# A recurrence in six head pairs: T ahead of U in each level, an earlier half split, three k-steps moved into the preparation, other wait counts

## The reference

```python
def step(S, inp):
    r_t, d_t, k_t, v_t, kk_t, b_t = inp
    sa = jnp.einsum('bhij,bhj->bhi', S, -kk_t)
    S = S * d_t[:, :, None, :] + sa[..., None] * b_t[:, :, None, :] + v_t[..., None] * k_t[:, :, None, :]
    return S, jnp.einsum('bhij,bhj->bhi', S, r_t)
...
decay = jnp.exp(-jnp.exp(w))
b = kk * a
...
gates = jax.nn.sigmoid((mg + gate_b).astype(jnp.float32)).reshape(B, S, N_BRANCH, D_MODEL)
```

## Time and profile before

| | us |
|---|---|
| median of 3 runs (range) | 3747.38 (3745.06 to 3751.47) |
| the profiled execution, device time | 3744.87 |
| its span, from the first to the last instruction | 3743.1 |
| PE busy | 3579.6 (96%) |
| DVE, ACT, POOL busy | 2261.2, 1618.1, 434.4 |
| chain that ended last, PE's share | 83% |
| mean granted clock of TensorE | 0.984 |

### The profile page before, as it was taken

One profiled execution on the slowest core, in us unless ns is written; L12 is line 12 of the kernel. 1 busy time (PEld: TensorE's weight loads), 2 busy tenths in 40 slices (PEclk: granted clock), 3 DMA queues, 4 the chain that ended last, 5 costly groups with the idle time before them and its releaser, 6 DMA issues.

```text
span 3743.1 us, 84941 instructions
## 1 busy us (share of the span) xinstructions
PE 3579.6 (96%) x33038; PEld 3520.4 (94%) x33038; DVE 2261.2 (60%) x3089; ACT 1618.1 (43%) x2173; POOL 434.4 (12%) x481
## 2 busy tenths in 40 slices
PE   6999999999999999899999999999999699999996
PEld 6999888889999999889999999999999699999996
DVE  6787666665565477876545454566665554545454
ACT  4456433244444434654434343443444343434343
POOL 5000232300010000312000000020002500000007
PEclk9999999999999999999999999999999899999998
DMA  5544222235655555445555555555455355555553
GB/s 200 164 149 146 92 70 70 77 112 184 200 183 184 186 170 169 147 152 181 182 184 177 190 177 184 178 185 185 158 164 164 111 185 177 189 179 184 177 189 124
DMA packets 165422, 606.24 MB, mean 162 GB/s; under 512 B 18384, under 2 KB 18512, under 8 KB 164992
## 3 DMA queue, kind: packets, MB, share of 16 engines
q1 hardware_dynamic: 163296, 594.62, 49.4%
q10 hardware_dynamic: 1760, 6.80, 0.5%
q0 software_dynamic: 192, 2.23, 0.2%
HBM read 601.47 MB, written 2.10 MB: 161 GB/s over the span
## 4 chain that ended last, share of the span: by engine, by line
PE 83%; DVE 9%; POOL 3%; ACT 2%; issue 2%; ACTq 0%; DVEq 0%; POOLq 0%
PE bank L313 26%; PE bank L314 26%; PE bank L315 25%; PE bank L1187 4%; DVE w_lo L302 2%; POOL ln_acc L2517 1%; POOL ln_acc L2520 1%; POOL ln_d L2515 1%; POOL ln_sq L2518 1%; ACT w_hi L293 0%; ACT X L2557 0%; DVE hx L372 0%; DVE mem_hl L372 0%; DVE xa L1765 0%; PE bank L1393 0%
## 5 line engine op out<-in xcount | busy, mean ns | idle before, releaser
L293 ACT ACTIVATE w_hi<-raw 128x1024 fp32r<-128x1024 f32 x1130 | 1162.1, 1052 | 974.7 <-PE bank L315 957.5
L302 DVE TENSOR_TENSOR w_lo<-raw,w_hi 128x1024 fp32r<-128x1024 f32 x1130 | 1375.0, 1256 | 101.2 <-ACT w_hi L293 101.0
L313 PE MATMUL bank<-u,w_hi 128*128 128x256 f32 (+1 forms) x2304 | 656.9, 285 | 9.6 <-DVE w_lo L302 9.5
L314 PE MATMUL bank<-u,w_hi 128*128 128x256 f32 (+1 forms) x2304 | 658.7, 286 | 0.0
L315 PE MATMUL bank<-u,w_lo 128*128 128x256 f32 (+1 forms) x2304 | 657.5, 285 | 0.0
L313 PE MATMUL bank<-hid,w_hi 128*128 128x256 f32 x2048 | 579.8, 283 | 0.0
L314 PE MATMUL bank<-hid,w_hi 128*128 128x256 f32 x2048 | 579.6, 283 | 0.0
L315 PE MATMUL bank<-hid,w_lo 128*128 128x256 f32 x2048 | 579.6, 283 | 0.0
L313 PE MATMUL bank<-xh,w_hi 128*128 128x256 f32 x1808 | 514.7, 285 | 18.3 <-issue 15.3
L314 PE MATMUL bank<-xh,w_hi 128*128 128x256 f32 x1808 | 512.6, 284 | 0.0
L315 PE MATMUL bank<-xh,w_lo 128*128 128x256 f32 x1808 | 512.6, 284 | 0.0
(11 more groups left out here) (447 smaller groups left out, 5667.7 us busy)
## 6 DMA issues: line engine op xcount, KB each, us to landing
raw<-stream SPq DMA_DIRECT2D x1130, 512.0 KB, 4.1
x_raw<-xT ACTq DMA_DIRECT2D x4, 512.0 KB, 10.4
mem_raw<-memT ACTq DMA_DIRECT2D x4, 512.0 KB, 18.2
x_res<-xT POOLq DMA_DIRECT2D x1, 2048.0 KB, 8.5
out<-X SPq DMA_DIRECT2D x4, 512.0 KB, 2.6
cst<-consts ACTq DMA_DIRECT2D x1, 1504.0 KB, 15.0
w_sb<-w ACTq DMA_DIRECT2D x1, 384.0 KB, 19.8
a_sb<-a ACTq DMA_DIRECT2D x1, 384.0 KB, 19.6
```

What stands on the lines that cost most here:

```text
L293: nc.scalar.activation(w_hi[:, slot], raw[:, slot], ACT.Copy).then_inc(hi_ready, 1)
L302: nc.vector.tensor_tensor(w_lo[:, slot], raw[:, slot], w_hi[:, slot].bitcast(F), ALU.subtract).then_inc(lo_ready, 1)
L313: nc.tensor.matmul(dst, w_hi[:, slot, j], hi, start=first, stop=False)
L314: nc.tensor.matmul(dst, w_hi[:, slot, j], lo, start=False, stop=False)
```

## The change

Five edits, all in the recurrence stage.

1. In each level PE makes T first and then U. DVE waits for T, adds it, waits for U, adds it. ACT's copy of the next X waits for the count of U, which is now the later one.
2. The first half of tile 2 ("the third weight tile") is split at the start of the round: by ACT ahead of the first tanh, by DVE as its first instruction. The second half stays where both were.
3. `GO_PREP` goes from 24 to 27 and `GO_GRAM` from 7 to 6. The sum of the k-steps is the same, and from the levels on their places too.
4. The first k-step of tile 0 waits for one count of `gate_kept` less (pairs 1 to 5), so for the third gate of the pair before and not for the fourth. In pair 0 tiles 0 and 1 do not wait for it. For tiles 1, 2 and 3 of the other pairs the count is what it was.
5. The number of computing instructions is the same. On DVE the first four levels have one wait more for each direction.

```diff
-GO_START, GO_PREP, GO_GRAM, GO_STEP = 8, 24, 7, 1
+GO_START, GO_PREP, GO_GRAM, GO_STEP = 8, 27, 6, 1
...
-                        + [f"{n}{l}_{d}" for d in D2 for n in (("U", "T") if l < LEVELS - 1 else ("U",))]]
+                        + [f"{n}{l}_{d}" for d in D2 for n in (("T", "U") if l < LEVELS - 1 else ("U",))]]
...
                     if kt == 0:
-                        pe.wait_ge(gate_kept, p * BESIDE + max(k // KT - 1, 0))
+                        if p > 0 or k >= 2 * KT:
+                            pe.wait_ge(gate_kept, p * BESIDE + k // KT - 1)
...
             with act.Fori(0, PAIRS) as p:
+                split_hi(act, pair_tile(p, 0).later(), (0,))
...
-                split_hi(act, pair_tile(p, 0).later())
+                split_hi(act, pair_tile(p, 0).later(), (1,))
                 split_hi(act, pair_tile(p, 1).later())
...
-                            need(act, rw_p, f"T{l - 1}_{d}", p)
+                            need(act, rw_p, f"U{l - 1}_{d}", p)
...
             with v.Fori(0, PAIRS) as p:
+                split_lo(v, pair_tile(p, 0).later(), (0,))
...
-                dve_pair_tile(v, p, 0)
+                dve_pair_gate(v, p, 0)
+                split_lo(v, pair_tile(p, 0).later(), (1,))
...
-                        else:
-                            need(v, rw_p, f"U{l}_{d}", p)
+                        need(v, rw_p, f"U{l}_{d}", p)
...
-                        rw_p.done(each(bank_of(d, 2), w["x"], w["u"]), f"U{l}_{d}")
                         if l < LEVELS - 1:
                             rw_p.done(each(bank_of(d, 0), w["u"], w["x"]), f"T{l}_{d}")
+                        rw_p.done(each(bank_of(d, 2), w["x"], w["u"]), f"U{l}_{d}")
```

## The result

| | before | after |
|---|---|---|
| median of 7 runs, us | 3747.77 (3744.77 to 3751.47) | 3760.66 (3756.7 to 3763.0) |
| ratio | | 1.0032, 95% interval 1.0021 to 1.0043 |
| span of the profiled execution, us | 3743.1 | 3758.8 |

The change makes the kernel slower by 0.32%. Of the 15.7 us by which the spans differ, 14.4 lie between the first pair's low-rank product and the first product behind the last pair's levels (398.97 to 749.93 before, which is 350.96; 398.07 to 763.43 after, 365.36).

What follows compares the result with a forecast made beforehand. PE, busy 96% of the span, was taken as the bound, so its idle time and clock count. 3744.87 + 3.4 + 11.5 = 3759.8 us, stated as 3761; forecast range 3755 to 3768, 8 in 10 range 3748 to 3788.

Steps and rivals of the forecast that it cites:

- The new wait: Tile 2's first k-step waits for DVE's read of tile 0: 3.25 us idle a pair, 6.9 in pair 0; +11.7.
- The start of a pair: At the start of pairs 1 to 5 PE no longer waits for the fourth gate: 0.75 us each, -3.8.
- Levels: T before U shortens four levels by 0.12 us each and their end by 0.26: 0.75 a pair, -4.5.
- The clock: In the stage PE falls to half clock after the wait: 9.0 us in five pairs, 2.5 in pair 0, +11.5.
- Without the clock: Recurrence stage: 11.7 us for the wait, -3.8 for the pair starts, -4.5 for the levels, together +3.4.
- A: Stage clock stays up after the wait in pairs 1 to 5, only pair 0 pays: 3753 us, chance 0.22.
- B: Stage clock stays down long behind the wait, each fall costing 6.4 us: 3785 us, chance 0.18.
- C: DVE and POOL overlap less, so PE's gap shrinks towards today's two waits: 3738 us with 2.1 saved, chance 0.10.
- D: Making T before U gains nothing in the levels: +4.5 us, so 3767 us, chance 0.08.

Runs made afterwards that it cites:

- the filler: Changed kernel with 7 unused 128x128 products of 256 columns put on PE ahead of k-step 32 in each pair: 3752.07 us, ratio 1.0013 to the kernel before.

## Why the prediction was right, point by point

It gave 3761 and slower; measured are 3760.7. The mechanism was right: the wait, the queue behind it, its length and the clock behind it. That the number is within 0.3 us is in part luck. The gain of the levels was put 1.6 us too high and the cost of the clock some 1.7 too high, and the two cancel. The sum was 3759.8; 1.2 were added because the median lay above the profiled execution, and 1.3 came in outside the stage, for which there was no term.

- **The new wait.** Foreseen 3.25 in pairs 1 to 5 and 6.9 in pair 0; the trace has 3.23 or 3.24 and 6.85. The undoing of the move (3734) and the earlier read (3732) show that the queue behind the waiting k-step is the cause. The table load was hidden as said, and DVE's row kept its length: from its first instruction to the end of the read it took 11.42 (467.02 to 478.44) for 11.44, and `bb` of direction 1 took 0.94 for 0.96.
- **The start of a pair.** Foreseen -0.75 five times, -3.8; alone it gave -3.8 by the medians, with an interval from -7.5 to -0.7.
- **Levels.** This term was mis-sized: -4.5 foreseen, and the trace of T ahead of U alone gives 0.5 a pair, about -3 (by the medians -2.5, not told from nothing). The end of the levels gave what was foreseen; the four levels gave 0.2 a pair for 0.48. Named was the floor of 1.16 by ACT's copy. It is 1.19 in levels 2 to 5, and the start of a run of products behind a wait, 0.05, was left out.
- **The clock.** Foreseen 9.0 in pairs 1 to 5; the filler prices it at 7.8 in the trace and 8.6 in the medians. Four of the five waits there were followed by a fall, for 6/7 assumed, at 1.9 each, for 2.1. In pair 0 PE was busy 3.94 us at half clock, and half of that is 2.0 (an estimate), for 2.5. The chance of 6/7 was counted from gaps of 2.8 us and more. The same trace has two of 2.28 and 2.27 that were followed by half clock too, so that 2.45 in pair 0 left the clock up did not say where such gaps begin.
- **Without the clock** the stage was to grow by 3.4. In the filler's trace it grew by 6.7 (357.67 for 350.96), about 1.7 of it for the fall in pair 0 that is left, so 5.0; the 1.6 of the levels account for the difference.
- **Rivals.** A (the clock stays up) was right for pair 5 alone. B (a long fall) is wrong: in pair 0 the clock came back at 419.42, in the middle of the small products, and no fall of the stage was longer than 6.83. C (the gap shrinks) did not happen, as DVE and POOL kept their overlap. D (the reorder does nothing) is wrong in the trace: the waits for `u` are gone, and two thirds of the 4.5 came. Its time had a slip: 3761 and 4.5 are 3765.5, not 3767.

Outside the stage the changed kernel loses 1.3 us more, 0.9 less ahead of it and 2.2 more behind it. There the idle place of 3.17 that did not bring the clock down before does now, and PE is busy for 2.91 us at half clock, which costs about 1.5 (half of it, an estimate). No run took the rest apart.

## What to carry to other kernels

An early operand is no gain while a second wait of the same instruction comes last: list all that an instruction waits for before moving it, and look at what is queued behind it. In an in-order queue move the instruction that ends the wait (here one read of 0.42 us, up by some 4 us) and not the one that waits. In this kernel an idle place of some 3 us on TensorE cost its length and then, most times, 1.4 to 2.5 us more by the clock, so one wait of 3.2 is worse than two of 0.9 by more than the 1.5 us of its additional length.

## What was not expected of the hardware

- The same idle gap brings the clock down or not: 3.23 in pair 5 did not, 3.23 and 3.24 in pairs 1 to 4 did, 3.17 did in one execution and not in another, and 2.67 in pair 0 of the kernel with the early read, with one of 0.47 close behind it, did. Ahead of the stage a gap of 2.28 did, in the kernel before (PE, and the stretch at half clock that follows), while 2.45 in pair 0 did not. What decides it was not tried. For an estimate, a fall is therefore a chance for each gap and not a price.

```profile
55.09 0.36 PE L313 MATMUL bank<-hx,w_hi 128*128 128x256 f32 x1 [2.28 <-DVE w_lo L302]
```

```profile
55.91:59.32 3.41, 3.41 (x19) 3.41 (x18) 3.41 (x5) 0.00 (x0) 3.17 (x4) 0.50 0.83 277
```

- The clock came back while small products of 64x64 ran, in pairs 0 and 1, while in the stretch at 776.12, whose products are 128x128 with 64 columns, it had not for 13.65 us. What tells the two apart was not tried.
- A full-precision product of 128x128 with 256 columns shows as two records of 0.216 us each at full clock, so it costs 3.6 times one of the three products of a k-step (0.12).
